# Gated delta rule in a hybrid encoder: the next tile pair's first transposes and masks moved ahead of this pair's finished inverse and state update

## The reference, cut to what matters

```python
def chunk_gated_delta(q, k, v, g, beta):
    ...
    L = jnp.where(strict, jnp.einsum('bhnid,bhnjd->bhnij', kb, k) * decay, 0.0)
    A = L + jnp.eye(C, dtype=jnp.float32)
    tri = lambda rhs: lax.linalg.triangular_solve(A, rhs, left_side=True, lower=True,
                                                  unit_diagonal=True)
    u = tri(vb)
    w = tri(kb * jnp.exp(gc)[..., None])
    attn = jnp.einsum('bhnid,bhnjd->bhnij', q, k) * decay
    def step(state, inp):
        ...
        v_new = u_i - jnp.einsum('bhcd,bhde->bhce', w_i, state)
        o = (jnp.einsum('bhcd,bhde->bhce', q_i * jnp.exp(gc_i)[..., None], state)
             + jnp.einsum('bhij,bhje->bhie', attn_i, v_new))
        ...
        state = state * jnp.exp(g_last)[..., None, None] + jnp.einsum('bhcd,bhce->bhde', k_dec, v_new)
        return state, o
```

## Time and profile before

| | us |
|---|---|
| median of 3 runs | 1118.73 (1118.71 to 1119.53) |
| profiled execution, time | 1119.67 |
| its span, first to last instruction | 1117.9 |
| PE busy in the span | 1063.5 (95%) |
| DVE busy | 529.2 (47%) |
| ACT busy | 378.2 (34%) |
| POOL busy | 123.6 (11%) |
| mean granted TensorE clock | 0.977 |

### The profile page before, as it was taken

The page is one execution under the profiler, slowest core; times in us unless marked ns, Lnnn a source line. Parts: engine busy times, 40 slices in busy tenths (PEclk is TensorE's granted clock), DMA queues, the critical chain, the costliest instruction groups (busy, mean ns, idle before and its releaser), DMA issues.

```text
span 1117.9 us, 14281 instructions
## 1 busy us (share of the span) xinstructions
PE 1063.5 (95%) x5878; PEld 895.2 (80%) x5878; DVE 529.2 (47%) x745; ACT 378.2 (34%) x563; POOL 123.6 (11%) x199
## 2 busy tenths in 40 slices
PE   8899999989998889899999999989999999999995
PEld 7789798767777778787888888878888888888884
DVE  5784446566666666645524335263332333322314
ACT  5444545654332212144323222153232322311212
POOL 4000000614762331000000000000000000000000
PEclk9899999999998999899999999989999999999998
DMA  9313320000010010411333324523324243232301
GB/s 303 103 47 114 112 68 2 1 1 11 4 22 6 1 39 11 142 38 57 113 94 94 113 64 181 151 66 86 107 81 113 76 113 88 101 113 87 104 18 75
DMA packets 104000, 87.18 MB, mean 78 GB/s; under 512 B 13109, under 2 KB 93697, under 8 KB 103936
## 3 DMA queue, kind: packets, MB, share of 16 engines
q1 hardware_dynamic: 102288, 81.80, 24.2%
q0 software_dynamic: 1488, 4.40, 1.1%
q10 hardware_dynamic: 160, 0.07, 0.0%
HBM read 83.64 MB, written 2.62 MB: 77 GB/s over the span
## 4 chain that ended last, share of the span: by engine, by line
PE 86%; DVE 7%; ACT 2%; issue 2%; DMA 1%; POOL 1%; SPq 0%; DVEq 0%; ACTq 0%; POOLq 0%
PE psum L887 22%; PE psum L889 22%; PE psum L888 22%; PE psum L1015 3%; PE psum L1033 3%; PE psum L1214 2%; PE psum L1023 2%; PE psum L1241 1%; PE psum L1297 1%; PE psum L1285 1%; PE psum L1166 1%; DVE Zx L1874 1%; PE psum L1152 1%; DVE Xm L1874 1%; PE psum L1086 1%
## 5 line engine op out<-in xcount | busy, mean ns | idle before, releaser
L887 PE MATMUL psum<-hT_hi,w_hi 128*128 128x512 f32 (+1 forms) x712 | 280.5, 394 | 7.5 <-DVE w_lo L1874 5.8
L889 PE MATMUL psum<-hT_hi,w_lo 128*128 128x512 f32 (+1 forms) x712 | 279.0, 392 | 0.0
L888 PE MATMUL psum<-hT_lo,w_hi 128*128 128x512 f32 (+1 forms) x712 | 279.0, 392 | 0.0
L1874 DVE TENSOR_TENSOR w_lo<-w_raw,w_hi 128x2048 fp32r<-128x2048 f32 (+2 forms) x81 | 167.4, 2067 | 231.1 <-ACT w_hi L1452 231.1
L1452 ACT ACTIVATE w_hi<-w_raw 128x2048 fp32r<-128x2048 f32 (+2 forms) x82 | 141.3, 1724 | 163.5 <-PE psum L889 151.6
L887 PEld LDWEIGHTS psum<-hT_hi,w_hi 128*128 128x128 f32 (+1 forms) x712 | 134.6, 189 | 37.7 <-DVE w_lo L1874 7.1
L889 PEld LDWEIGHTS psum<-hT_hi,w_lo 128*128 128x128 f32 (+1 forms) x712 | 134.4, 189 | 28.9
L888 PEld LDWEIGHTS psum<-hT_lo,w_hi 128*128 128x128 f32 (+1 forms) x712 | 134.5, 189 | 28.1
L1874 DVE TENSOR_TENSOR psum<-gate_act,psum 128x512 f32<-128x512 f32 x22 | 15.3, 696 | 120.4 <-PE psum L889 120.4
L887 PE MATMUL psum<-w_hi,act_hi 128*128 128x512 f32 x176 | 68.5, 389 | 0.0
L888 PE MATMUL psum<-w_lo,act_hi 128*128 128x512 f32 x176 | 68.5, 389 | 0.0
(11 more groups left out here) (297 smaller groups left out, 1628.8 us busy)
## 6 DMA issues: line engine op xcount, KB each, us to landing
w_raw<-in_w_in_dram SPq DMA_DIRECT2D x23, 1024.0 KB
w_raw<-in_ffn_w_gate_up_dram SPq DMA_DIRECT2D x44, 512.0 KB
w_raw<-in_ffn_w_down_dram SPq DMA_DIRECT2D x10, 1024.0 KB
w_raw<-in_mem_w_kv_dram SPq DMA_DIRECT2D x4, 1024.0 KB
w_raw<-in_w_out_dram SPq DMA_DIRECT2D x4, 1024.0 KB
x_tok<-in_x_dram SPq DMA_DIRECT2D x4, 512.0 KB, 5.3
w_raw<-in_w_branch_mla_dram SPq DMA_DIRECT2D x4, 512.0 KB
w_raw<-in_w_branch_dn_dram SPq DMA_DIRECT2D x4, 512.0 KB
```

What stands on the lines that cost most here:

```text
L887: pe.matmul(o, s_hi, m_hi, start=first, stop=False)
L888: pe.matmul(o, s_hi, m_lo, start=False, stop=False)
L889: return pe.matmul(o, s_lo, m_hi, start=False, stop=last)
L1874: return dve.tensor_tensor(o, a, b, op)
```

## The change

PE: `first_inverse(g+1)` moves from the head of pair `g+1` to pair `g`'s level 6, behind `level_second(g, 6)` and ahead of `scan_update(g-1)` and `pairs("A", g, 1)`. DVE: the X1 masks of pair `g+1` move ahead of `inverse_done(g)`, `scan_update(g-1)` and `scores(g, 1)`. For the last pair DVE's order becomes `scan_update`, `prep(("z", 0))`, `inverse_done`, `scores`; before, it was `prep(("z", 0))`, `inverse_done`, `scan_update`, `scores`. ACT, POOL, SP and the turn of the PSUM banks stay as they are.

```diff
@@ PE
             for g in range(NT):
                 last = g - 1
-                first_inverse(g)
                 if g == 0:
+                    first_inverse(0)
                     turn_out(NT - 1)
...
                     if s == 6:
+                        if g + 1 < NT:
+                            first_inverse(g + 1)
                         if last >= 0:
                             scan_update(last)
                         pairs("A", g, 1)
@@ DVE
-                for p in range(2):
-                    masked(("X1", g, p), g, p, FIRST)
+                if g == 0:
+                    for p in range(2):
+                        masked(("X1", 0, p), 0, p, FIRST)
...
-                    if g == NT - 1 and s == 6:
-                        prep(("z", 0))
-                inverse_done(g)
-                if last >= 0:
+                if g + 1 < NT:
+                    for p in range(2):
+                        masked(("X1", g + 1, p), g + 1, p, FIRST)
+                    inverse_done(g)
+                    if last >= 0:
+                        scan_update(last)
+                    scores(g, 1)
+                else:
                     scan_update(last)
-                scores(g, 1)
+                    prep(("z", 0))
+                    inverse_done(g)
+                    scores(g, 1)
```

## The result

| | before | after |
|---|---|---|
| first measurement, median | 1118.74 us | 1104.69 us (1102.5 to 1106.51) |
| ratio | | 0.9876, interval 0.986 to 0.9892 |
| measured again together, median | 1118.08 | 1104.8 (1100.0 to 1106.74) |
| ratio | | 0.9886, interval 0.9866 to 0.9907 |
| profiled execution, time and span | 1119.67, 1117.9 | 1104.05, 1102.3 |

The change is faster by 1.1 to 1.2%, 13.3 to 14.1 us, where 10.6 were forecast.

A forecast was written before the change was run, and what follows sets the result against it. PE was taken as the bound of the delta rule, waiting on DVE's order and then running at half clock. Gains 3.1 + 3.7 + 3.8 + 0 = 10.6 us gave 1108.1 us from the median footing; range 1105.0 to 1112.0.

The forecast's parts named there:

- DVE's order ended the border wait: At border 2 to 3, PE waits 2.98 us because DVE does other passes before the mask, not for DVE's total work.
- The three borders: Between tile pairs, moved transposes and masks let PE start earlier: gains of 3.1, 3.7 and 3.8 us.
- The waits for `Zs`: PE's new stalls at the moved transposes: 1.4 and 0.6 us at the first border, 0.3 and 0.6 at others.
- `T` cost: At the first border DVE is late with `T`, so PE stalls 1.3 us there.
- Rivals 3, 4 and 5: DVE becomes bound (1112.2 us, 0.10); PE parks at moved transposes (1122.7, 0.03); mask wait not DVE's order, no change (1118.7, 0.02).
- rival 2: At the tail, the clock holds despite the wait: 1105.4 us, chance 0.08.
- no half clock at the first border: Border 0 to 1: with only 8 transposes in PE's gap, the clock stays full and the border gives 3.1 us.
- the 1.5 us that it implied: First border: if transposes don't count as busy, the clock drops and the summed gain is some 1.5 us smaller.
- Gain 0: Tail, pair 3 to z tiles: the wait moves behind one group at similar length, half clock expected again; 0 us gained.
- The old one cost ... 2.7 us. New start of the z tiles: 456.15 + 1.8 + 2.7: Tail: the old wait's 2.7 us slow-work cost is charged again, so z tiles start at 460.65, as before.
- After 466 us PE's work is a queue of weight products; it shifts as a whole: Behind the tail, PE's remaining work moves with the schedule as one block; no gain or loss counted there.
- The bounds of the tail (0.7 lost to 2.7 gained): Tail: 2.7 us gained if the clock stays full, 0.7 lost if DVE is a pass later.

The follow-up runs named there:

- pe_only: Kernel before with only TensorE's half of the change: X1 transposes early, DVE's masks where they were; 1117.89 us, ratio 1.0005.
- borders_only: The change at the three borders on both engines, with DVE's old order behind pair 3, against the kernel before; 1107.17 us, ratio 0.9908.
- later_8: Kernel before plus eight TensorE products ahead of z_tile(0), written over by the real ones; time moved by +0.1 us, ratio 0.9997.
- filled_wait: Kernel before in its old order, last pairs multiplied two or three times and X1 transposes of pairs 1 to 3 done twice; 1108.36 us, ratio 0.992.

## Why the prediction was wrong in size

**Right, at their place.** DVE's order ended the border wait: pe_only gained nothing. The three borders came out at 3.1, 3.7 and 3.8 us in the profile, as forecast, and at 10.9 together in borders_only for 10.6. That the sum met the first profile to a tenth is in part luck: the second profile of the kernel before would give 10.3, and that of later_8, with its second border at full clock, 7.7. The waits for `Zs` were as counted, 1.4 and 0.5 us at the first border and 0.2 and 0.5 at the others; `T` cost 1.0 and not 1.3; DVE ran without slack into level 5 and lost about 0.1 us to it. Rivals 3, 4 and 5 did not occur, nor did rival 2: the tail's clock did drop.

**Right: no half clock at the first border.** It was 1.00 there in all three profiles of the changed kernel. The rule of the Trainium skill ("TensorE: Matmul & The Clock Gate", Part 4: PE-mode transpose) that transposes do not count as PE being busy would have made that gap idle; the trace does not bear out the 1.5 us that it implied. This alone does not refute the rule, since pe_only passed a wait of 2.76 us, with no work in it, at full clock. More against it is later_8's second border: eight transposes and then 2.95 us of waiting, and the clock stayed at 1.00. Filling the waits partly with transposes worked as well, though pairs were added at the same time.

**Wrong: the tail, "Gain 0".** The schedule was right, and so was the expectation of half clock: `scan_queries(3)` waited 3.31 us for that `attT`, where 3.5 were forecast. The step that failed is "The old one cost ... 2.7 us. New start of the z tiles: 456.15 + 1.8 + 2.7": it gave waits of equal length an equal price ("I take 0, as the waits are equally long"). The new wait was followed by half clock for 3.4 us and not 6.8, in all three profiles, which cost 1.7 us for 2.7; pe_only shows the old one costing nothing once. Without slow time the two tails are equal: 18.48 − 1.7 = 16.8 us after, and 16.8 in pe_only, which has the old order. So "Gain 0" was right for the schedule, and this step is 1.0 us of the miss.

**Wrong: "After 466 us PE's work is a queue of weight products; it shifts as a whole".** It shifted, and the 2.3 us wait near 517 was no longer followed by half clock: 1.6 us. The runs with added products show that a shift alone can do this. The prediction had read that stretch as having no part in the change, since nothing in it is touched. The bounds of the tail (0.7 lost to 2.7 gained) knew only the clock at the tail itself. With the 1.0 and the 1.6, the forecast sum is 13.2 for 13.3 measured in the repetition. The remainder of the first measurement's 14.1 us lies within the spread of executions, 5 us for the kernel before.

**Open.** Why the new tail order lets the wait near 517 pass at full clock and the old one doesn't isn't settled. The shifts show that timing plays a part and not only the wait's length; they don't give a rule by which it could have been counted.

## What to carry to other kernels

Price a PE wait of 2 to 3.5 us twice: the wait, and the slow work that may follow; here the second part was the larger, 6.0 of 10.7 us. Before reordering anything, give PE redundant work in such a wait: that took a few lines and brought 9.7 us, 8.7 of them in the waits that were filled. When a stretch moves in time, expect untouched short waits behind it to gain or lose a microsecond or two each (here 1.6 and 2.5), and put that into the range; and follow a freed wait to the next resource (here `state`, then `attT`'s bank, then the z tile's bank) before stopping.

## What the runs showed of the hardware

- Waits of the same length were followed by half clock or not: 2.76 us without and 2.79 with it in one execution; 3.46 us with in before and without in pe_only; 2.33 us with in one kernel, without in another. The tail's wait had half clock behind it for 6.8 us in before (3.46 us of waiting) and for 3.4 us in after (3.31).
- Waits of 1.2 to 1.9 us at the borders, where filled_wait had shortened them from 2.7 to 3.0, left the clock at 1.00. Two short ones with 0.66 us of work between them, 2.0 and 1.4 near 740 us, were followed by half clock in some kernels and not in others.
- More work made the kernel faster: 0.9 us of added products, 1.0 us less time (the interval, 0.9978 to 0.9999, only just excludes none); filled waits, 9.7 us less.
- Executions of one kernel differ by up to 5 us (1114.7 to 1120.0 for the kernel before), and where two profiles of the changed kernel differ, it is ahead of the change (341.64 for 338.98 us).
